# Recurrent block of a hybrid decoder: recurrent and gate units interleaved, each tile's gate chain one tile behind its convolution

## What is computed

```
gate_br, rnn_br = split(x @ w_in_c, 2)                    # 1024 -> 2 x 1024
xc = causal_dwconv(rnn_br, width 4)
r = sigmoid(xc_block @ w_gate_a + b_gate_a)               # 8 blocks of 128 x 128
i = sigmoid(xc_block @ w_gate_x + b_gate_x)
log_a = 8 * r * log_sigmoid(lambda);  a = exp(log_a)
b = sqrt(1 - a^2) * (i * xc);  h_t = a_t * h_{t-1} + b_t  # along the tokens
y = (gelu(gate_br) * h) @ w_out_c
```

## Time and profile before

| | us |
|---|---|
| median of 3 runs (lowest, highest) | 1567.96 (1567.31, 1568.05) |
| the profiled execution, its own time | 1568.38 |
| its span | 1566.6 |
| TensorE busy | 1458.7 |
| VectorE busy | 866.3 |
| ScalarE busy | 616.2 |
| mean granted clock of TensorE | 0.968 of full |

### The profile page before, as it was taken

How to read it: one execution, slowest core, us unless ns; L and a number is a source line. 1 busy time by engine, 2 the same in 40 slices (tenths; PEclk the granted TensorE clock), 3 DMA queues, 4 the chain that set the end, 5 groups by cost and what they waited for, 6 DMA issues and landing times.

```text
span 1566.6 us, 24363 instructions
## 1 busy us (share of the span) xinstructions
PE 1458.7 (93%) x10352; PEld 1423.4 (91%) x10352; DVE 866.3 (55%) x1266; ACT 616.2 (39%) x943; POOL 21.4 (1%) x32
## 2 busy tenths in 40 slices
PE   6999999999699999999999698887899999999993
PEld 6999898989699999999999597876899999999992
DVE  4555564546665544543446777866755445534555
ACT  4342524333353314331333547943633133313333
POOL 0010100000000000000000000000000000000000
PEclk9999999999799999999999799999999999999997
DMA  6131222213122221222222021111122222222211
GB/s 244 41 110 56 85 81 70 83 56 110 41 68 81 82 95 68 81 95 81 69 71 92 27 90 46 54 67 55 54 82 81 90 73 82 81 84 79 75 62 76
DMA packets 34781, 122.10 MB, mean 78 GB/s; under 512 B 3952, under 2 KB 4080, under 8 KB 34416
## 3 DMA queue, kind: packets, MB, share of 16 engines
q1 hardware_dynamic: 32112, 111.63, 20.5%
q0 software_dynamic: 2560, 8.91, 2.0%
HBM read 112.83 MB, written 7.70 MB: 77 GB/s over the span
## 4 chain that ended last, share of the span: by engine, by line
PE 81%; DVE 8%; ACT 7%; issue 2%; DMA 1%; SPq 0%; DVEq 0%; ACTq 0%
PE PS L422 25%; PE PS L423 25%; PE PS L424 24%; PE PS L493 2%; DVE Y L1111 1%; DVE Y L1108 1%; ACT whi L640 1%; DVE xlo L1119 1%; PE PS L579 1%; PE PS L531 1%; DMA C<-consts 1%; DVE S L1031 1%; PE PS L511 1%; PE PS L546 1%; ACT L865 1%
## 5 line engine op out<-in xcount | busy, mean ns | idle before, releaser
L422 PE MATMUL PS<-xhi,whi 128*128 128x296 f32 x2176 | 667.9, 307 | 47.3 <-DVE xlo L1119 31.0
L423 PE MATMUL PS<-xlo,whi 128*128 128x296 f32 x2176 | 658.3, 303 | 0.0
L424 PE MATMUL PS<-xhi,wlo 128*128 128x296 f32 x2176 | 655.3, 301 | 0.0
L422 PEld LDWEIGHTS PS<-xhi,whi 128*128 128x128 f32 x2176 | 416.1, 191 | 56.2 <-DVE xlo L1119 35.7
L423 PEld LDWEIGHTS PS<-xlo,whi 128*128 128x128 f32 x2176 | 416.0, 191 | 1.1 <-issue 0.2
L424 PEld LDWEIGHTS PS<-xhi,wlo 128*128 128x128 f32 x2176 | 415.2, 191 | 0.0
L422 PE MATMUL PS<-hhi,whi 128*128 128x296 f32 x960 | 288.5, 301 | 8.6 <-ACT S L875 7.5
L900 DVE TENSOR_TENSOR wlo<-raw,whi 128x1024 fp32r<-128x1024 f32 (+1 forms) x198 | 238.2, 1204 | 96.1 <-ACT whi L640 92.5
L423 PE MATMUL PS<-hlo,whi 128*128 128x296 f32 x960 | 288.9, 301 | 0.0
L424 PE MATMUL PS<-hhi,wlo 128*128 128x296 f32 x960 | 287.6, 300 | 0.0
L640 ACT ACTIVATE whi<-raw 128x1024 fp32r<-128x1024 f32 (+1 forms) x198 | 206.5, 1043 | 180.2 <-PE PS L424 166.0
(11 more groups left out here) (196 smaller groups left out, 1135.2 us busy)
## 6 DMA issues: line engine op xcount, KB each, us to landing
raw<-weights SPq DMA_DIRECT2D x182, 512.0 KB, 3.2
raw<-weights SPq DMA_DIRECT2D x16, 384.0 KB, 2.9
Y<-xT SPq DMA_DIRECT2D x8, 296.0 KB, 9.7
yT<-Y SPq DMA_DIRECT2D x8, 296.0 KB, 2.1
S<-s_hgrn POOLq DMA_DIRECT2D x4, 512.0 KB, 4.8
S<-s_ret POOLq DMA_DIRECT2D x4, 512.0 KB, 5.7
hgrn_out<-S POOLq DMA_DIRECT2D x4, 512.0 KB, 3.9
ret_out<-S POOLq DMA_DIRECT2D x4, 512.0 KB, 3.9
```

The costliest lines, as they stand in the source:

```text
L422: pe.matmul(dst, wh, h, start=first, stop=False)
L423: pe.matmul(dst, wh, lo, start=False, stop=False)
L424: return pe.matmul(dst, wl, h, start=False, stop=last)
```

## The change

The sixteen units of `w_in_c` are put in one order, `MIXER`: r0, r1, g0, r2, g1, r3, g2, and so on to r7, g6, g7, with r for a recurrent and g for a gate unit. The weight stream is laid in that order. `gates_after(i)` says after which unit of the list the gate products of which tile run: tile 0 after g0, tile 1 after r2, tile m from 2 to 7 after g(m-1), which is one unit after r(m). Each engine's list is written as one loop over `MIXER`:
- TensorE runs the unit, then the gate products if there are any.
- ScalarE copies the weights two units ahead, evacuates the unit (`branch` or `gelu`), then for the tile of `gates_after`: gate tanh, the high part of the last product (`mix_high`), and exp, tanh and root (`decay`).
- VectorE takes the weight difference, convolves (`convolve`) or multiplies by the GELU (`gated`), then runs `log_a` and `recurrence` of that tile to its end, scan and copies with it. The eight-column product with h0 now comes ahead of the wait for the root.
- `gelu` waits for `h_lo` of the tile before, since it writes the row that `mix_low` reads; the product is now written in place, in the GELU's row. The convolution has one scratch row, not two; `S` has eleven rows for ten.

```diff
--- before.py
+++ after.py
@@ -52,8 +52,7 @@
 U_FFN0 = U_OUTAB + KT
 N_FFN = 2 * FT + KT * len(GROUPS)
 U_RNN = U_FFN0 + N_FFN
-U_GBR = U_RNN + KT
-U_OUTC = U_GBR + KT
+U_OUTC = U_RNN + 2 * KT
 U_FFN1 = U_OUTC + KT
 U_ALL = U_FFN1 + N_FFN
@@ -71,6 +70,22 @@
 FFN = ffn_order()
+
+
+def mixer_order():
+
+    order = [("r", 0)]
+    for m in range(1, KT):
+        order += [("r", m), ("g", m - 1)]
+    return order + [("g", KT - 1)]
+
+
+MIXER = mixer_order()
+
+
+def gates_after(i):
+
+    return {2: 0, 3: 1}.get(i, i // 2 if i % 2 == 0 and i > 3 and i // 2 < KT else None)
@@ -213,7 +228,7 @@
         hlo = sb("hlo", [P, KT, T], F32R)
         at_stage = schedule()
         Y = sb("Y", [P, KT, T])
-        S = sb("S", [P, 10, SCRW])
+        S = sb("S", [P, 11, SCRW])
         V = sb("V", [P, 2, BLK + 1, P])
         KV = sb("KV", [P, BLK + 1 + NB, P])
@@ -600,11 +615,7 @@
                 gemm(U_OUTAB + m, hhi, hlo)
             layer_norm_moments(0)
             ffn(0)
-            gemm(U_RNN, xhi, xlo, x_lo, 2 * KT, both=True)
-            for m in range(2, KT):
-                gemm(U_RNN + m, xhi, xlo)
-            pe.wait_ge(gw_loaded, 16)
-            for m in range(KT):
+            def gates(m):
                 pe.wait_ge(xc_ok, m + 1)
                 if m:
                     pe.wait_ge(gate_sb, 2 * m)
@@ -613,9 +624,13 @@
                         mm = pe.matmul(PS[:, 4 + 2 * g + half, 0:HT], GW[:, g * D + m * P:g * D + m * P + P],
                                        Y[:, m, half * HT:half * HT + HT], start=True, stop=True)
                     mm.then_inc(gate_ps, 1)
-                if m:
-                    gemm(U_GBR + m - 1, xhi, xlo)
-            gemm(U_GBR + KT - 1, xhi, xlo)
+
+            gemm(U_RNN, xhi, xlo, x_lo, 2 * KT, both=True)
+            pe.wait_ge(gw_loaded, 16)
+            for i in range(2, len(MIXER)):
+                gemm(U_RNN + i, xhi, xlo)
+                if gates_after(i) is not None:
+                    gates(gates_after(i))
             gemm(U_OUTC, hhi, hlo, h_lo, FT, both=True)
             for m in range(2, KT):
                 gemm(U_OUTC + m, hhi, hlo)
@@ -825,10 +840,7 @@
             layer_norm(0)
             ffn(0)
-            act.wait_ge(pads, 2)
-            for m in range(KT):
-                u = U_RNN + m
-                weights_hi(u + 2)
+            def branch(u, m):
                 wait_full(u)
                 if m >= 2:
                     act.wait_ge(xc_ok, m - 1)
@@ -844,6 +856,7 @@
                 done(act.activation(out_small("lc_p", m * n, n), a[:, 1, NP - HT - n:NP - HT], ACT.Copy))
                 done(act.activation(batches(out_small("lc_s", m * NB * n, NB * n)), smp[:, :, NS - n:], ACT.Copy),
                      free[u % 2], u // 2 + 1)
+
             def gates_of(m):
                 for g in range(2):
@@ -851,29 +864,43 @@
                     done(act.activation(halves(s(gate_row(m, g))), PS[:, 4 + 2 * g:6 + 2 * g, 0:HT], ACT.Tanh,
                                         scale=0.5, bias=lam[:, (5 + g) * KT + m:(5 + g) * KT + m + 1]), gate_sb)
-            def mix_high(m):
-                act.wait_ge(hmul, m + 1)
-                done(act.activation(hhi[:, m, :], s(8), ACT.Copy), h_hi)
-
-            act.wait_ge(half_b, 1)
-            act.wait_ge(xc_ok, KT)
-            gates_of(0)
-            for m in range(KT):
-                weights_hi(U_GBR + m + 2)
+            def decay(m):
+
                 r = s(gate_row(m, 0))
                 act.wait_ge(la, m + 1)
                 done(act.activation(s(a_row(m)), r, ACT.Exp))
                 done(act.activation(r, r, ACT.Tanh, scale=-1.0), aa)
-                if m:
-                    mix_high(m - 1)
-                if m + 1 < KT:
-                    gates_of(m + 1)
                 act.wait_ge(w2, m + 1)
                 done(act.activation(r, r, ACT.Sqrt, scale=0.25), mult)
-                u = U_GBR + m
+
+            def gelu(u, m):
                 wait_full(u)
-                done(act.activation(halves(s(7)), acc[u % 2][:, :, 0:HT], ACT.Gelu_apprx_tanh), free[u % 2], u // 2 + 1)
-            mix_high(KT - 1)
+                if m:
+                    act.wait_ge(h_lo, FT + m)
+                done(act.activation(halves(s(GEL)), acc[u % 2][:, :, 0:HT], ACT.Gelu_apprx_tanh),
+                     free[u % 2], u // 2 + 1)
+
+            def mix_high(m):
+                act.wait_ge(hmul, m + 1)
+                done(act.activation(hhi[:, m, :], s(GEL), ACT.Copy), h_hi)
+
+            act.wait_ge(pads, 2)
+            act.wait_ge(half_b, 1)
+            for i, (kind, m) in enumerate(MIXER):
+                weights_hi(U_RNN + i + 2)
+                g = gates_after(i)
+                if kind == "r":
+                    branch(U_RNN + i, m)
+                    if i == 3:
+                        mix_high(0)
+                else:
+                    gelu(U_RNN + i, m)
+                if g is not None:
+                    gates_of(g)
+                if kind == "g" and m:
+                    mix_high(m)
+                if g is not None:
+                    decay(g)
             for m in range(KT):
                 weights_hi(U_OUTC + m + 2)
                 squares(U_OUTC + m, m)
@@ -1222,10 +1249,11 @@
             for r in range(2):
                 done(dve.memset(S[:, r, 0:CW - 1], 0.0), pads if r else None)
-            for m in range(KT):
-                weights_lo(U_RNN + m + 2)
+            first = slice(NP, T, NS)
+
+            def convolve(m):
                 dve.wait_ge(u_sb, FT + m + 1)
-                r, t = S[:, m % 2, :], S[:, 2 + m % 2, :]
+                r, t = S[:, m % 2, :], S[:, 2, :]
                 n = LU - CW + 1
                 done(ts(t[:, 0:n], r[:, 0:n], par("conv_w_c", m), par("conv_b_c", m), ALU.mult, ALU.add))
                 for q in range(1, CW - 1):
@@ -1237,7 +1265,6 @@
                 def tail(row):
                     return row[:, q + NP:LU].rearrange("p (b s) -> p b s", b=NB)
                 done(stt(batches(Y[:, m, NP:T]), tail(r)[:, :, q:], w, tail(t)[:, :, 0:NS], ALU.mult, ALU.add), xc_ok)
-            first = slice(NP, T, NS)
             def log_a(m):
                 dve.wait_ge(gate_sb, 2 * m + 2)
@@ -1246,34 +1273,44 @@
                 done(ts(r, r, 1.0, lam[:, KT + m:KT + m + 1], ALU.add, ALU.mult), la)
                 done(stt(i, i, 1.0, Y[:, m, :], ALU.add, ALU.mult))
+            def recurrence(m):
+                r, i, a = s(gate_row(m, 0)), gate_row(m, 1), a_row(m)
+                dve.wait_ge(aa, m + 1)
+
+                done(tt(s(SCAN), s(a), s(a), ALU.mult))
+                done(stt(r, s(SCAN), 1.0, r, ALU.add, ALU.mult), w2)
+                if m:
+                    mix_low(m - 1)
+                t8 = lbc[:, 0:NB]
+                done(tt(t8, S[:, a, first], par("h0", m * NB, NB), ALU.mult))
+                dve.wait_ge(mult, m + 1)
+                done(tt(s(i), s(i), r, ALU.mult))
+                done(tt(S[:, i, first], S[:, i, first], t8, ALU.add))
+                done(dve.memset(S[:, a, first], 0.0))
+                done(dve.tensor_tensor_scan(s(SCAN), s(a), s(i), 0.0, ALU.mult, ALU.add))
+                done(dve.tensor_copy(out_small("h_p", m, 1), S[:, SCAN, NP - 1:NP]))
+                done(dve.tensor_copy(out_small("h_s", m * NB, NB), S[:, SCAN, NP + NS - 1:T:NS]))
+
+            def gated(u, m):
+                free_of(u)
+                done(tt(s(GEL), s(SCAN), s(GEL), ALU.mult), hmul)
+
             def mix_low(m):
                 dve.wait_ge(h_hi, FT + m + 1)
-                done(tt(hlo[:, m, :], s(8), hhi[:, m, :].bitcast(F32), ALU.subtract), h_lo)
-
-            log_a(0)
-            for m in range(KT):
-                weights_lo(U_GBR + m + 2)
-                r, i, a = s(gate_row(m, 0)), gate_row(m, 1), a_row(m)
-                dve.wait_ge(aa, m + 1)
-
-                done(tt(s(5), s(a), s(a), ALU.mult))
-                done(stt(r, s(5), 1.0, r, ALU.add, ALU.mult), w2)
-                if m + 1 < KT:
-                    log_a(m + 1)
-                if m:
-                    mix_low(m - 1)
-                dve.wait_ge(mult, m + 1)
-                done(tt(s(i), s(i), r, ALU.mult))
-
-                t8 = lbc[:, 0:NB]
-                done(tt(t8, S[:, a, first], par("h0", m * NB, NB), ALU.mult))
-                done(tt(S[:, i, first], S[:, i, first], t8, ALU.add))
-                done(dve.memset(S[:, a, first], 0.0))
-                done(dve.tensor_tensor_scan(s(6), s(a), s(i), 0.0, ALU.mult, ALU.add))
-                free_of(U_GBR + m)
-                done(tt(s(8), s(6), s(7), ALU.mult), hmul)
-                done(dve.tensor_copy(out_small("h_p", m, 1), S[:, 6, NP - 1:NP]))
-                done(dve.tensor_copy(out_small("h_s", m * NB, NB), S[:, 6, NP + NS - 1:T:NS]))
+                done(tt(hlo[:, m, :], s(GEL), hhi[:, m, :].bitcast(F32), ALU.subtract), h_lo)
+
+            for i, (kind, m) in enumerate(MIXER):
+                weights_lo(U_RNN + i + 2)
```

(22 more changed lines are left out.)

## The result

The changed kernel takes 1577.0 us (1574.6 to 1578.2, four runs) against 1568.0 (1567.3 to 1568.6): the ratio is 1.0065, with an interval of 1.0049 to 1.0082, so it is slower by 7.7 to 12.9 us. The forecast was 1584, range 1577 to 1592.

A forecast was written before the change was run, and what follows sets the result against it. The prediction took a serial cross-engine loop of 18.13 us per tile to bound the new block, against 15.1 of TensorE work. From the profiled 1568.4 us, +12.5 for the block and +3 for the clock gave 1584, range 1577 to 1592.

The forecast's parts named there:

- case A: Interleaved block: the loop bounds, the clock falls after few or no new waits; 1578 to 1588 us, chance 0.77.
- part 2: Gate values of one tile to the next, through ScalarE, VectorE and TensorE: a serial loop of 18.13 us.
- part 3: TensorE's idle times over the whole block, ends included: 30.7 us for 17.6; block taken as 12.5 us longer.
- the layout: Block laid out instruction by instruction with traced durations; ends at 161.5 us in the new order, 149.7 in the old.
- the second part: TensorE's work per tile, two units of 6.54 us and gates of 2.01: 15.1 us, against 16.67 before.
- Part 1: Busy time per tile in the new order: ScalarE 12.6 us, VectorE 13.1, both under TensorE's 15.1.
- part 4: Half clock at the gates after five new TensorE waits of 2.6 to 3.0 us: about 0.6 each, +3 us.
- Rival B: VectorE between root and gates: convolutions come in time and TensorE bounds; 1554 us, chance 0.05 faster, 0.04 level.
- rival C: Gates: each 3 us wait drops the clock, loop 20.3 us; 1591.6 us, or 1588 where half come early; chance 0.14.
- the signs named ahead: Trace signs: gates wait 21 to 25 us for convolutions, scan pitch 18, 5 us weight-difference wait, ScalarE idle about 2 per tile.

The follow-up runs named there:

- e1: Changed kernel without VectorE's scan over the tokens; products after it read the squared a instead. 1565.8 us, ratio 1.0002 to the kernel before.
- e6: e3 plus filler: TensorE computes four gate products, later overwritten, before waiting for the convolution, from tile 2 on. 1580.4 us, ratio 1.0092.
- e2: Changed kernel plus one extra VectorE product per tile, placed where VectorE waits for the square root. 1579.3 us, ratio 1.0079.
- e4: The split kernel: changed kernel with square root and recurrence tail moved to the next unit's place, behind evacuation and next convolution. 1549.0 us, ratio 0.9884.
- e3: Changed kernel plus one extra VectorE product per tile, behind the recurrence's copies, ahead of weight difference and convolution. 1587.6 us, ratio 1.0135.
- e7: Changed kernel with only VectorE's order altered: from tile 3, weight difference and convolution precede the previous recurrence's tail. 1573.0 us, ratio 1.0050.
- e8: e4 plus filler gate products on TensorE at tile 3 alone, before its wait for the convolution. 1550.2 us, ratio 0.9895.
- e5: Changed kernel plus filler: TensorE computes four gate products, later overwritten, before waiting for the convolution, from tile 2 on. 1577.5 us, ratio 1.0061.

## Why the prediction was right

The mechanism was right and the size was not. The forecast was 16 us more and 9 were measured; 1577.0 stands on the lower end of the range (1577 to 1592) and under the bounds that case A gave itself (1578 to 1588). That it still lies inside is luck, not precision.

- **The loop** (part 2) held to the hundredth: 18.13 us forecast, 18.13 to 18.14 measured from scan to scan of tiles 3 to 5 and 6 to 7, where the clock stayed up (19.38 where it fell). Its terms held too: VectorE's stretch from the root to the end of the convolution was 7.63 us forecast and is 7.63 (978.34 to 985.97). e1 and e6 show that this stretch counts in full (the scan and its gap out, 1.42 us less pitch; the product in, 0.81 more at full clock), and e2 that the wait for the root covers what is put there. The loop's other terms were read from the trace and not varied one by one.
- **The waits** (part 3): forecast 2.6, 1.5, 9.3, four of 3.03 and 5.2, in all 30.7 us; measured 1.46, 1.33, 8.89, then 1.92, 2.77, 2.78, 2.35, and 5.07, in all 26.6. With a wait of 2.77 the pitch is 18.14, so 15.37 us pass from restart to the next wait, where the split kernel does the same work without a wait in 15.10. These 0.27 us stand in no wait: the gates take 2.26 us after a wait for 2.15 without one, and the last matmul ahead of a wait counts as busy for its whole 0.30 us, where in a stream the next one starts 0.14 us after it. Three of the waits differ for other causes. Tile 2's is shorter by 1.1 us: the first GELU's table load, laid behind the wait for its unit, ran ahead of it (900.32, the GELU at 903.31), and with the load behind the wait tile 0's gate values would have come some 0.8 us later. Tiles 4 and 7 come behind the slow gates of tiles 3 and 6, which made TensorE late as well. One load of weights, that of unit 4, was late by 0.15 us, where the layout had none late.
- **TensorE's need** of 15.1 us per tile (the second part) is what e4 reached: 15.10. Part 1's busy times hold for 10 us and not for the pitch of 10.13 us, which puts them 0.1 us low; nothing rests on it (e4 has 12.9 us of VectorE and 12.6 of ScalarE in 15).
- **The clock** (part 4) was mis-sized. It was taken as 0.6 us at each of five waits, +3; in the profiled execution it fell at one of them (1004.17, gates 3.51 us for 2.26), and the gates took 1.3 us longer. So the mean over five was 0.25 us; the term was a guess between two bounds, and nothing in the rows said which wait would bring a fall.
- **The total** is 1577, 7 us under the forecast. Between the two profiled executions (1568.4 and 1577.1) it is 8.8 us where the forecast had 12.5 + 3 = 15.5. Inside the block 12.5 us were measured with the fall of the clock in them, so some 11.2 without it: the clock term was 1.7 us too large and the layout's +12.5 about 1.3 (the layouts as wholes gave 11.8, the closer figure). The remaining 3.7 us lie outside the block: the stretches before and after it came out 2.2 and 1.5 us shorter, though they run the same instructions. Executions differ by as much there whatever the kernel: ahead of the block all ten kernels of this document run the same work, and in their profiles the recurrent unit that first waits for ScalarE starts at 893.7 to 898.7 us, with 844.2 to 849.5 us of busy TensorE ahead of it; the kernel before had the latest start. Its own time ran from 1563.0 to 1569.5 us in the later runs. The forecast added its terms to one profiled execution and had no term for that.
- **Rival B** (the convolutions come in time) fell, and so did **rival C** for this kernel. e3 shows C's mechanism: with waits of 3.58 us the clock fell each time. It cost 1.5 us a tile, not 2.13, in a loop that was 0.81 us longer by the added product; that its pitch of 20.46 is near C's 20.3 is chance. The 1588 that C gives where half of the falls come early follows from no sum that it shows.

Of the signs named ahead, the gates' waits came to 20.2 us, just under the 21 to 25 given, over six waits with the longest 8.89, ScalarE waits 1.77 us per tile for the root's argument, and the GELU wait gave way to one of 5.07 us for the weight difference.

The table load stayed at 1.3 us per switch (971.76, exp from 973.05). The rule of the Trainium skill (ScalarE: Activation LUTs, What ACT_TABLE_LOAD costs), some 2.66 us for a switch, would by an estimate from that figure make the pitch 20.9; the trace does not agree with it.

## What to carry to other kernels

Before interleaving two phases to fill an engine, look whether some engine's own list puts the new producer behind a chain of waits, and add up the loop across engines, not the busy time of each alone (here 12.6 and 13.1 us of busy time fitted in 15.1, and the loop was 18.1). Where a chain goes to another engine and back, cut it at the way back and put the rest one unit later; here doing so on both engines turned +9 us into -18, and on VectorE alone it gained at most a few us. An engine's waits that are harmless while another bounds become part of the loop once the loop bounds. A forecast that adds terms to one execution carries that execution's own deviation, here some 4 us, in its range or not at all.

## What the runs showed of the hardware

- The length of a wait alone does not tell whether TensorE's clock is down, in part or in whole, in the gates behind it. It was after waits of 2.27 (e3, tile 2, gates 3.95 us), 2.77 (e2, tile 5), 2.78 (changed kernel), 2.93 (e7) and 3.14 us (e8), and it was not after 2.35, 2.77 (both changed kernel), 2.77 (e2, tile 7) and 2.92 (e7). After the three of 3.58 us in e3 it was each time. Gates behind such a fall took 3.1 to 4.3 us for 2.2. With filler matmuls, which left waits of at most 1.94 us at the gates of tiles 4 to 7, it stayed up (e6, e5), but not behind the longer wait of tile 3 (6.89 in e5, 7.71 in e6, 3.14 in e8).
- The GELU's table load, which before the change came only after the wait for the unit, ran ahead of that wait in the changed kernel and in e4 (load 972.10, GELU 973.75 after a wait of 0.37). The root's load still waited for its argument (changed kernel, 976.25 after 1.77), and exp's for log a (e4, 906.80 after 0.64). Why the one moved was not tried; from tile 3 on it lies off the loop.

```profile
972.10 1.28 ACT L889 ACT_TABLE_LOAD   x1
973.75 0.67 ACT L889 ACTIVATE S<-PS 128x592 f32<-128x592 f32 x1 [0.37 <-PE PS L444]
```
